# Final norm moved into the last four expert steps, expert loop in groups of step pairs: a 1-core encoder step

## The chip, the cores and the metric

One core of a Trainium2 chip runs the whole program. The metric is device time in microseconds (us). The kernel before took 2573.78 us (median of 3 runs, 2573.71 to 2576.18).

## What is computed

One layer for a prompt (2048 tokens) and a batch of samples (8 x 16 tokens), width 1024, float32: token mixing, cross-attention, a mixture of 32 SwiGLU experts, and a final RMSNorm. The part around the change, cut from the reference:

```
def rms_norm(x, g):
    y = x * lax.rsqrt(jnp.mean(x * x, axis=-1, keepdims=True) + EPS)
    return y * g

# top-1 of 4 groups, then top-2 of the 8 experts of that group
expert = g_idx * EXPERTS_PER_GROUP + top_i            # (n, 2)
y = routed_experts(t, expert, w_eg, w_eu, w_ed)       # silu(x @ w_eg[e]) * (x @ w_eu[e]) @ w_ed[e]
x = x + einsum('nk,nkd->nd', gate, y)
...
y_prompt = rms_norm(xp, g_final)
y_sample = rms_norm(xs, g_final)
```

Both experts of a token are in one group of eight.

## The kernel before

The 2176 tokens are 17 tiles of 128 rows (tile 0 in the order of work is the sample tile, then the 16 prompt tiles). The program is a row of stages; each ends with a barrier of all engines and a clearing of its semaphores (`one_stage`, L108 to L117). The last two concern us.

The router and expert stage (L1257 on). For each tile it makes x2 (input plus attention) and the normed h3, stores both to DRAM (`x2_d`, `h3_d`), routes the tokens, and writes for each of a token's two experts one row [token, gate] into `table_d` at a place that depends on expert and rank (`place`, `scatter_slots`). Then it runs the expert steps. A step has two lanes of 64 rows: the upper half of the array's columns works for an expert of 0 to 15, the lower half for one of 16 to 31 (`both`, L1992). Weights lie in three slots of 6 MB; lane 0 alternates between two, lane 1 has one, so that its next expert is loaded part by part (gate, up, down; 2 MB each, `load_part`, L1245) as the step that used it last frees each part. The loads are in the order of need on SP's queue.

In a step (`work` of each engine), TensorE multiplies gate and up, turns the next step's input (`turn_x`) and its own hidden rows (`turn_h`), and multiplies down. ScalarE does silu, half of each eviction and half of the output (`y_evac`, L1646); VectorE does the other halves. GpSimd gathers the input rows two steps ahead (`gather`, L1505), reads the pairs [token, gate] three steps ahead (`fetch`) and once more for the output (`fetch_again`), and adds the 128 output rows onto `x2_d` with an indirect accumulating DMA (`scatter`, L1515), each after the one before has landed (semaphores `y_out`).

How many steps are needed (`ns`) is known only on the device, between 34 and 84. `expert_steps` (L1370) runs steps 1 to 3 and then a loop of 40 pairs with an `If(t.v < ns)` around each step: L91 is the loop, L1378 the two conditions. In this run `ns` is 42 (steps 0 to 41): 19 pairs of the loop work and 21 are passed over.

The final norm (L2146 on) is a stage of its own: SP loads the 17 tiles of x2 (L2165), ScalarE squares and sums them (L2192), GpSimd makes rstd in two instructions (L2177, L2179), VectorE scales (L2204), SP and ScalarE store (L2169, L2187).

## Time and profile before

| | |
|---|---|
| median of 3 runs | 2573.78 us |
| the profiled execution | 2574.19 us |
| its span, first to last instruction | 2572.3 us |
| TensorE matmul busy | 2441.5 us, 95% of the span |
| VectorE, ScalarE, GpSimd busy | 859.4, 467.1, 510.7 us |
| DMA moved | 391.12 MB, mean 152 GB/s |
| expert steps | 1 to 41 from about 1573 to 2501 us, 22.62 us each |
| final stage, with what leads to it | 2501 to 2572 us |

The page divides the span into 40 slices of 64 us. TensorE stands at nine tenths or more in nearly all of them and at 8 and 0 in the last two, where DMA is at 4 and 7. So there is one stretch where the engine that bounds the program has nothing to do, and it is the end. The table says nothing of waits: those are read in the timeline.

### The profile page before, as it was taken

How to read it: one execution, taken by the hardware profiler on the slowest of the kernel's cores; microseconds unless marked ns; L12 is line 12 of the kernel's file. 1: busy time of each engine (PE TensorE's matmuls, PEld its weight loads, DVE VectorE, ACT ScalarE, POOL GpSimd, SP SyncE). 2: the span in 40 equal slices, each digit the busy share in tenths (PEclk: the TensorE clock that was granted, in tenths of full speed). 3: DMA queues.
4: the chain of work that ended last, by engine and by line, in shares of the span. 5: the costliest groups of instructions: out<-in, count | busy, mean ns of one | idle time of the engine just before them, and what ended most of it. 6: DMA issues, size and time to landing. Idle time of an engine off the chain costs nothing. (4 is left out here: it accounts for less than half of the span.)

```text
span 2572.3 us, 30380 instructions
## 1 busy us (share of the span) xinstructions
PE 2441.5 (95%) x9511; PEld 1120.5 (44%) x9512; DVE 859.4 (33%) x2312; ACT 467.1 (18%) x945; POOL 510.7 (20%) x623
## 2 busy tenths in 40 slices
PE   8999999999999988999999999999999999999980
PEld 4444444444444664555555543333333333333330
DVE  1586747566584212233333332111111111110113
ACT  2222222222121122222222211001010101010103
POOL 1122222322222000011111112211222221222214
PEclk9999999999999999999999999999999999999995
DMA  6211011110243325311111147945987297988947
GB/s 222 103 45 52 33 62 37 62 37 33 87 156 123 119 108 211 133 65 65 66 66 66 58 156 238 331 128 169 296 291 245 49 326 245 304 283 267 311 145 288
DMA packets 154278, 391.12 MB, mean 152 GB/s; under 512 B 20738, under 2 KB 21274, under 8 KB 154186
## 3 DMA queue, kind: packets, MB, share of 16 engines
q1 hardware_dynamic: 133666, 339.57, 37.1%
q0 software_dynamic: 19040, 45.23, 7.3%
q10 hardware_dynamic: 1488, 5.26, 0.5%
q8 instruction: 46, 0.75, 0.1%
q14 instruction: 38, 0.31, 0.0%
HBM read 323.53 MB, written 66.71 MB: 152 GB/s over the span
## 5 line engine op out<-in xcount | busy, mean ns | idle before, releaser
L1994 PE MATMUL r_pss<-W,r_h2T 128*64 x1312 | 571.2, 593 | 1.0 <-issue 1.0
L1995 PE MATMUL r_pss<-W,r_h2T 128*64 128x512 f32 x1312 | 571.2, 593 | 0.0
L748 PE MATMUL a_psz<-W 128*128 128x512 f32 x1088 | 481.1, 595 | 1.3 <-ACT W L506 1.3
L601 DVE SCALAR_TENSOR_TENSOR yacc<-aext,pcol,yacc 128x256 f32<-128x256 f32 x928 | 370.8, 476 | 0.3 <-issue 0.3
L1994 PEld LDWEIGHTS r_pss<-W,r_h2T 128*64 128x64 f32 x1312 | 180.0, 137 | 370.0 <-issue 370.0
L748 PEld LDWEIGHTS a_psz<-W 128*128 128x128 f32 x1088 | 203.6, 191 | 237.4 <-issue 237.4
L1994 PE MATMUL r_psx<-W,r_x1r 128*64 x656 | 290.1, 595 | 3.6
L1995 PE MATMUL r_psx<-W,r_x1r 128*64 128x512 f32 x656 | 290.3, 595 | 0.0
L1958 PE MATMUL r_psx<-W 128*128 128x512 f32 x544 | 237.6, 595 | 0.0
L1931 PE MATMUL r_pss<-W,r_h2T 128*128 128x512 f32 x512 | 226.9, 596 | 3.1 <-POOL r_tokens L1449 3.1
L1805 DVE TENSOR_TENSOR r_x1r<-r_pss,r_x1r 128x256 f32<-128x256 f32 x84 | 31.7, 419 | 530.4 <-PE r_pss L1995 504.5
L1515 POOL DMA_INDIRECT x_scratch<-r_x,e_stoken x42 | 69.4, 1653 | 643.2 <-DVE r_x L1817 319.2
L1995 PEld LDWEIGHTS r_pss<-W,r_h2T 128*64 128x64 f32 x1312 | 180.2, 137 | 0.0
L471 POOL TENSOR_TENSOR W<-W 128x512 f32<-128x512 f32 x34 | 115.3, 3397 | 268.1 <-ACT W L578 268.1
L1994 PEld LDWEIGHTS r_psx<-W,r_x1r 128*64 128x64 f32 x656 | 86.5, 137 | 174.1 <-issue 174.1
L1958 PEld LDWEIGHTS r_psx<-W 128*128 128x128 f32 x544 | 102.6, 191 | 122.6 <-issue 122.6
L1931 PEld LDWEIGHTS r_pss<-W,r_h2T 128*128 128x128 f32 x512 | 95.4, 191 | 111.5 <-issue 111.5
L916 PE MATMUL a_psz<-W,a_maT 128*128 128x512 f32 x272 | 122.3, 592 | 0.0
L916 PE MATMUL a_psz<-W 128*128 128x512 f32 x272 | 122.3, 592 | 0.0
L1817 DVE TENSOR_SCALAR r_x<-r_psx,e_spair 128x512 f32<-128x512 f32 x42 | 31.5, 750 | 260.5 <-PE r_psx L1995 258.3
L1995 PEld LDWEIGHTS r_psx<-W,r_x1r 128*64 128x64 f32 x656 | 86.5, 137 | 0.0
L1630 ACT ACTIVATE r_x1r<-r_pss 128x512 f32<-128x512 f32 x42 | 25.1, 597 | 322.8 <-PE r_pss L1995 322.7
(337 smaller groups left out, 2246.6 us busy)
## 6 DMA issues: line engine op xcount, KB each, us to landing
W<-in_w_expert_gate SPq DMA_DIRECT2D x32, 2048.0 KB, 10.8
W<-in_w_expert_up SPq DMA_DIRECT2D x32, 2048.0 KB, 9.6
W<-in_w_expert_down SPq DMA_DIRECT2D x32, 2048.0 KB, 10.6
W<-in_x_prompt SPq DMA_DIRECT2D x32, 512.0 KB, 4.2
x_scratch<-W SPq DMA_DIRECT2D x18, 512.0 KB, 3.0
r_x1r<-x_scratch SPq DMA_DIRECT2D x17, 512.0 KB, 4.3
x_scratch<-r_x SPq DMA_DIRECT2D x17, 512.0 KB, 2.9
h_scratch<-r_h SPq DMA_DIRECT2D x17, 512.0 KB, 2.9
```

Of the source, the lines that this page charges most:

```text
L471: pool.tensor_tensor(x, mixed[:, 512 * n:512 * n + 512], x, ALU.add).then_inc(S["x1_half"], 1)
L601: ins = dve.scalar_tensor_tensor(out=out, in0=src, scalar=w, in1=yacc[:, i, :], op0=ALU.mult, op1=ALU.add)
L748: last = pe.matmul(psz[bank][:], hT[t.par][:, k, :], w_in[bank][:, k, :], start=(k == 0), stop=(k == KD - 1))
L916: last = pe.matmul(psz[n][:], (maT[:, k, :] if k < CG else mbl[t.par][:, k - CG, :]), w_out[:, k, 512 * n:512 * n + 512], start=(k == 0), ...
L1515: pool.indirect_dma_start(out=x2_d.rearrange("t p d -> (t p) d"), out_offset=bass.IndirectOffsetOnAxis(ap=stoken[t.par][:], axis=0), in_=y ...
L1630: act.activation(sg[:], psg[:], ACT.Silu).then_inc(T["silu_done"], 1)
L1805: dve.tensor_tensor(hb[:, c], psu[:, c], sg[:, c], ALU.mult).then_inc(T["h_done"], 1)
L1817: dve.tensor_scalar(yb[t.par][:, 512:1024], psx[:, 512:1024], spair[t.par][:, 1:2], None, ALU.mult).then_inc(T["y_done"], 1)
L1931: last = pe.matmul(pss[:, 2 * n:2 * n + 2, :].rearrange("p h n -> p (h n)"), h2T[i % 2][:, k, :], A[:, k, 512 * n:512 * n + 512], start=(k ...
L1958: last = pe.matmul(psx[:, 512 * n:512 * n + 512], (pT if i else qT)[:, c, :], (B if i else w_xo)[:, c, 512 * n:512 * n + 512], start=(c == ...
L1994: pe.matmul(out[0:HALF, :], xt[:, 0:HALF], W[:, bass.ds(base + at, 512)], start=start, stop=stop)
L1995: return pe.matmul(out[HALF:P, :], xt[:, HALF:P], W[:, at:at + 512], start=start, stop=stop)
```

## The change

- Each row of `table_d` gets a third number: the row of the prompt output, or with 65536 added (out of range) if the token's other expert has a higher number. Of a token's two rows, only that of the later expert has a valid output row.
- Steps 1 to 3 as before. Then an outer loop over groups of 6 pairs, with a condition around the group, an inner loop over its pairs, and one condition around each pair. Then always four last steps, written out (j = 0 to 3). The device computes the number of pairs as (steps - 3) >> 1.
- In last step j ScalarE loads four tiles of x2 (behind its eviction of the next input, once all scatters of the steps before have landed), squares them in halves of 512 columns behind its half of the output eviction, and stores the normed tiles of round j-1 behind silu. VectorE adds the halves and eps and scales, in place. GpSimd makes rstd with one instruction. GpSimd's scatter of step j waits until the four loads of round j have landed.
- Tokens that one of the last four steps still changes are normed wrongly or too early in this. After the last scatter, GpSimd gathers the 4 x 128 rows of these steps again from `x2_d`, they are squared and scaled, and are written with an indirect DMA to the output rows of the third column, where out-of-range rows are dropped. The sample tile is loaded after the last scatter and normed whole.
- The final stage is gone; `g_final` is loaded by SP behind the third set of expert weights.

The core of the diff:

```
+LAST = 4
+ROUND = 4
+GROUP = 6
...
-        table_d = nc.dram_tensor("table_scratch", [NE * REG, 2], F32, kind="Internal").ap()
+        table_d = nc.dram_tensor("table_scratch", [NE * REG, 3], F32, kind="Internal").ap()
...
+            def count_pairs(eng):
                 eng.wait_ge(T["count_known"], 1)
-                return eng.value_load(count[0:1, 0:1], min_val=STEPS_MIN, max_val=STEPS_MAX)
-            def expert_steps(eng, ns, work):
-                def step(t):
-                    if isinstance(t.v, int) and t.v == 0:
-                        return
-                    if isinstance(t.v, int) and t.v < STEPS_MIN:
-                        work(t)
-                        return
-                    with eng.If(t.v < ns):
-                        work(t)
-                steps(eng, step, 4, (STEPS_MAX - 4) // 2, STEPS_MAX)
+                return eng.value_load(count[0:1, 0:1], min_val=(STEPS_MIN + 1 - LAST) // 2, max_val=(STEPS_MAX + 1 - LAST) // 2)
...
+            def expert_steps(eng, pairs, work):
+                for t in range(1, 4):
+                    work(fixed(t))
+                with eng.Fori(2, (STEPS_MAX + 1 - LAST) // 2, GROUP) as first:
+                    with eng.If(first < pairs):
+                        with eng.Fori(first, first + GROUP) as g:
+                            with eng.If(g < pairs):
+                                for u in range(2):
+                                    work(Tile(2 * g + u, g, u))
+                for j in range(LAST):
+                    work(Tile(2 * pairs + j, pairs + j // 2, j % 2), j)
...
+                    sp.wait_ge(S["h3_done"], NT)
+                    sp.dma_start(gl[:], I["g_final"].rearrange("(a d) -> a d", a=1).partition_broadcast(P).rearrange("p a d -> p (a d)")).then_inc(F["gl_here"], 16)
...
+                    pairs = count_pairs(sp)
+                    for i in range(2):
+                        sp.wait_ge(y_out[i], 16 * (pairs + LAST // 2))
+                        settle(sp)
+                    sp.wait_ge(T["h_turned"], 4 * (pairs + LAST // 2))
+                    settle(sp)
+                    sp.dma_start(sample[:], x2_d[1, :, :]).then_inc(F["sample_here"], 16)
+                    sp.wait_ge(F["out_done"], NT)
+                    sp.dma_start(O["y_s"].rearrange("b t d -> (b t) d"), sample[:]).then_inc(F["sample_out"], 16)
+                    sp.wait_ge(F["sample_out"], 16)
+                    for i in range(ROUND):
+                        sp.wait_ge(acc_out[i], 16 * LAST)
...
+                    pool.memset(place_f[:, 0, :], NOWHERE).then_inc(S["iotas"], 1)
+                    pool.iota(place_f[:, 1:NT, :], [[P, PT], [0, 2]], base=0, channel_multiplier=1, allow_small_or_imprecise_dtypes=True).then_inc(S["iotas"], 1)
...
                         need(pool, T["token_done"], t.v - 1)
+                        settle(pool)
                         fetch_pairs(t, pair[t.par], pair_here[t.par])
...
+                    pairs = count_pairs(pool)
+                    def final_rstd(n):
+                        pool.wait_ge(F["summed"], n + 1)
+                        pool.tensor_tensor(frs[:, n:n + 1], fsum[:, n:n + 1], mhalf[:], ALU.pow).then_inc(F["rstd"], 1)
+                    def work(t, j=-LAST):
+                        if j < LAST - 2:
+                            gather(t.at(2))
+                        if j < LAST - 3:
+                            fetch(t.at(3))
                         fetch_again(t)
+                        if j >= 0:
+                            pool.wait_ge(F["redo_known"], 2 * j + 2)
+                            for i in range(ROUND):
+                                pool.wait_ge(acc_here[i], 16 * (j + 1))
                         scatter(t)
-                    expert_steps(pool, ns, work)
+                        if j >= 0:
+                            for i in range(ROUND):
+                                final_rstd(ROUND * j + i)
+                    expert_steps(pool, pairs, work)
+                    final_rstd(PT)
                     for i in range(2):
-                        pool.wait_ge(y_out[i], 16 * ((ns + (1 - i)) // 2))
-                        pool.wait_ge(x_here[i], 16 * ((ns + (3 - i)) // 2))
-                        pool.wait_ge(pair_here[i], 32 * ((ns + (4 - i)) // 2))
+                        pool.wait_ge(x_here[i], 16 * (pairs + LAST // 2))
+                        settle(pool)
+                        pool.wait_ge(pair_here[i], 32 * (pairs + LAST // 2))
+                        settle(pool)
+                        pool.wait_ge(y_out[i], 16 * (pairs + LAST // 2))
+                        settle(pool)
+                    pool.wait_ge(T["x_turned"], 4 * (pairs + LAST // 2))
+                    settle(pool)
+                    pool.wait_ge(T["up_done"], 2 * (pairs + LAST // 2) + 1)
+                    settle(pool)
+                    for j in range(LAST):
+                        pool.indirect_dma_start(out=redo[j], out_offset=None, in_=x2_d.rearrange("t p d -> (t p) d"),
+                                                in_offset=bass.IndirectOffsetOnAxis(ap=redo_in[j][:], axis=0)).then_inc(redo_here[j], 16)
+                    for i in range(ROUND):
+                        pool.wait_ge(acc_out[i], 16 * LAST)
+                    final_rstd(NT)
+                    for j in range(LAST):
+                        if j + 1 < LAST:
+                            final_rstd(NT + j + 1)
+                        pool.wait_ge(F["out_done"], NT + j + 1)
+                        pool.indirect_dma_start(out=O["y_p"].rearrange("b t d -> (b t) d"),
+                                                out_offset=bass.IndirectOffsetOnAxis(ap=redo_out[j][:], axis=0),
+                                                in_=redo[j], in_offset=None, bounds_check=PT * P - 1, oob_is_err=False).then_inc(F["redone"], 16)
+                    pool.wait_ge(F["redone"], 16 * LAST)
...
+                    def final_load(j):
+                        for i in range(2):
+                            act.wait_ge(y_out[i], 16 * (pairs + (j + 1 - i) // 2))
+                            settle(act)
+                        if j == 0:
+                            act.wait_ge(S["h3T_done"], NT)
...
+                        for i in range(ROUND):
+                            need(act, acc_out[i], 16 * j)
+                            act.dma_start(acc[i], x2_d[2 + ROUND * j + i, :, :]).then_inc(acc_here[i], 16)
+                    def final_store(j):
+                        for i in range(ROUND):
+                            act.wait_ge(F["out_done"], ROUND * j + i + 1)
+                            act.dma_start(y_p[ROUND * j + i, :, :], acc[i]).then_inc(acc_out[i], 16)
+                    def square_f(n, src):
+                        for m in range(2):
+                            need(act, F["squares"], 2 * n + m)
+                            act.activation(junk_f, src[:, 512 * m:512 * m + 512], ACT.Square, scale=1 / 32,
+                                           accum_out=fss[:, n, m:m + 1]).then_inc(F["squares"], 1)
+                    def square_whole(n, src):
+                        need(act, F["squares"], PT + n)
+                        act.activation(pst[:].rearrange("p k n -> p (k n)"), src, ACT.Square, scale=1 / 32, accum_out=fss[:, n, 0:1]).then_inc(F["squares"], 1)
+                    def final_squares(j):
+                        for i in range(ROUND):
+                            act.wait_ge(acc_here[i], 16 * (j + 1))
+                            square_f(ROUND * j + i, acc[i])
+                    def work(t, j=-LAST):
                         silu(t)
+                        if j >= 1:
+                            final_store(j - 1)
                         hT_out(t)
-                        xT_out(t.at(1))
+                        if j < LAST - 1:
+                            xT_out(t.at(1))
+                        if j >= 0:
+                            final_load(j)
                         y_evac(t)
-                    expert_steps(act, ns, work)
+                        if j >= 0:
+                            final_squares(j)
+                    expert_steps(act, pairs, work)
+                    final_store(LAST - 1)
+                    act.wait_ge(F["sample_here"], 16)
+                    square_whole(PT, sample[:])
+                    for j in range(LAST):
+                        act.wait_ge(redo_here[j], 16)
+                        square_whole(NT + j, redo[j])
...
+                        for k in range(2):
+                            put(dve.tensor_tensor(sooner_f[par][:, k:k + 1], ef[par][:, k:k + 1], ef[par][:, 1 - k:2 - k], ALU.is_lt), "sooner")
+                        dve.wait_ge(S["sooner"], 2 * n)
+                        put(dve.scalar_tensor_tensor(out=val[par][:, :, 2], in0=sooner_f[par][:], scalar=NOWHERE, in1=place_f[:, i, :], op0=ALU.mult, op1=ALU.add), "rank2")
                         dve.wait_ge(S["slotf"], n)
-                        dve.wait_ge(S["rank2"], 2 * n)
+                        dve.wait_ge(S["rank2"], 3 * n)
                         put(dve.tensor_copy(slot_i[par][:], slotf[:]), "slot")
...
+                        if j >= 0:
+                            dve.tensor_copy(redo_in[j][:], spair[t.par][:, 0:1]).then_inc(F["redo_known"], 1)
+                            dve.tensor_copy(redo_out[j][:], spair[t.par][:, 2:3]).then_inc(F["redo_known"], 1)
...
+                    then(dve.tensor_tensor(most[:], end[0:1, EPL - 1:EPL], end[0:1, NE - 1:NE], ALU.max))
+                    then(dve.tensor_scalar(most_i[:], most[:], float(1 - LAST), None, ALU.add))
+                    dve.tensor_scalar(count[:], most_i[:], 1, None, ALU.arith_shift_right).then_inc(T["count_known"], 1)
...
+                    def final_sum(n):
+                        if n < PT:
+                            dve.wait_ge(F["squares"], 2 * n + 2)
+                            dve.tensor_scalar(fsum[:, n:n + 1], fss[:, n, 0:1], fss[:, n, 1:2], EPS, ALU.add, ALU.add).then_inc(F["summed"], 1)
+                        else:
+                            dve.wait_ge(F["squares"], PT + n + 1)
+                            dve.tensor_scalar(fsum[:, n:n + 1], fss[:, n, 0:1], EPS, None, ALU.add).then_inc(F["summed"], 1)
+                    def final_scale(n, tile):
+                        dve.wait_ge(F["rstd"], n + 1)
+                        if n == 0:
+                            dve.wait_ge(F["gl_here"], 16)
+                        dve.scalar_tensor_tensor(out=tile, in0=tile, scalar=frs[:, n:n + 1], in1=gl[:],
+                                                 op0=ALU.mult, op1=ALU.mult).then_inc(F["out_done"], 1)
+                    def work(t, j=-LAST):
+                        if j < LAST - 2:
+                            tokens(t.at(2))
                         hidden(t)
                         hT_out(t)
-                        xT_out(t.at(1))
-                        y_evac(t)
-                    expert_steps(dve, ns, work)
+                        if j < LAST - 1:
+                            xT_out(t.at(1))
+                        y_evac(t, j)
+                        if j >= 0:
+                            final_sum(ROUND * j)
+                            for i in range(ROUND):
+                                if i + 1 < ROUND:
+                                    final_sum(ROUND * j + i + 1)
+                                final_scale(ROUND * j + i, acc[i])
+                    expert_steps(dve, pairs, work)
+                    final_sum(PT)
+                    final_scale(PT, sample[:])
+                    final_sum(NT)
+                    for j in range(LAST):
+                        if j + 1 < LAST:
+                            final_sum(NT + j + 1)
+                        final_scale(NT + j, redo[j])
...
+                    def work(t, j=-LAST):
...
+                        more = j < LAST - 1
+                        if more:
+                            turn_x(t.at(1), (0, 1, 2, 3))
                         turn_h(t, 0)
-                        turn_x(t.at(1), (4, 5))
+                        if more:
+                            turn_x(t.at(1), (4, 5))
                         turn_h(t, 1)
-                        turn_x(t.at(1), (6, 7))
+                        if more:
+                            turn_x(t.at(1), (6, 7))
...
-        with one_stage() as st:
...
```

## Rows read from the trace of the kernel before

**Rows 1.** Windows; columns: stretch, its length, busy of each engine, PEclk, DMA share, GB/s.

```profile
2500.00:2524.00 24.00, 1.61 (x8) 0.30 (x4) 0.75 (x1) 0.69 (x1) 1.65 (x1) 0.58 0.15 22
2524.00:2572.00 48.00, 0.00 (x0) 0.00 (x0) 21.83 (x17) 19.54 (x34) 30.56 (x34) 0.50 0.96 383
```

**Rows 2.** Timeline, 2501 to 2567 us: start, length, engine, line, idle before in brackets.

```profile
2501.01 0.59 PE L1995 MATMUL r_psx<-W,r_x1r 128*64 128x512 f32 x1
...
2501.65 0.75 DVE L1817 TENSOR_SCALAR r_x<-r_psx,e_spair 128x512 f32<-128x512 f32 x1 [6.32 <-PE r_psx L1995]
...
2503.31 1.65 POOL L1515 DMA_INDIRECT x_scratch<-r_x,e_stoken  x1 [15.58 <-DVE r_x L1817]
...
2531.17 1.06 ACT L2192 ACTIVATE f_junk<-W 128x1024 f32<-128x1024 f32 x1 [0.30 <-DMA W<-x_scratch]
...
2564.30 0.57 POOL L2179 TENSOR_TENSOR f_rs<-f_rs,mhalf 128x1 f32<-128x1 f32 x1
...
2564.90 1.28 DVE L2204 SCALAR_TENSOR_TENSOR W<-W,f_rs,f_gfinal 128x1024 f32<-128x1024 f32 x1 [0.77 <-POOL f_rs L2179]
...
2566.21 0.34 SPq L2169 DMA_DIRECT2D out_y_s<-W  x1
```

**Rows 3.** Lines L1378 and L1382 after 2499.6 us: count, ns min/median/max, first and last start.

```profile
L1378 PEldq COMPARE_BRANCH  x38: 208/208/208, 2499.9 to 2520.4; - x38
...
L1378 POOLq COMPARE_BRANCH  x42: 45/45/50, 2503.5 to 2520.4; - x42
...
L1382 POOLq DRAIN  x1: 1621/1621/1621, 2521.6 to 2521.6; - x1
...
L1382 SPq EVENT_SEMAPHORE  x1: 17/17/17, 2523.4 to 2523.4; - x1
```

**Rows 4.** TensorE's queue at a pair boundary: start of a step's first issue and matmul.

```profile
L1994 PEldq FUSED_REGOPS  x6: 37/46/51, 2455.0 to 2456.2; - x6
...
L1994 PE MATMUL r_pss<-W,r_h2T x1: 592/592/592, 2456.2 to 2456.2; 128*64 x1
```

**Rows 5.** Windows of two clock drops, and of step 39; columns as in rows 1.

```profile
1514.20:1521.00 6.80, 4.99 (x15) 3.71 (x16) 3.47 (x16) 2.23 (x3) 1.85 (x2) 0.50 0.48 129
1558.50:1561.90 3.40, 3.40 (x10) 0.98 (x8) 0.90 (x4) 0.00 (x0) 1.13 (x2) 0.51 0.76 291
2433.57:2456.19 22.62, 22.49 (x111) 8.31 (x109) 2.65 (x7) 2.16 (x4) 4.86 (x6) 1.00 0.96 323
```

**Rows 6.** Timeline: TensorE's gap before 1515 us, and SP's last gate load.

```profile
1515.32 0.64 PE L1976 MATMUL r_psk<-r_picked,r_lower 128*128 128x32 f32 x2 [2.63 <-DVE r_picked L1749]
...
2441.01 0.39 SPq L1254 DMA_DIRECT2D W<-in_w_expert_gate  x1
```

**Rows 7.** DMA, 2441 to 2457 us: KB each, us from issue to landing.

```profile
W<-in_w_expert_gate SPq DMA_DIRECT2D x1, 2048.0 KB, 10.8
```

**Rows 8.** DMA by queue: packets, MB, share of 16 engines; 2539 to 2541 us.

```profile
q1 hardware_dynamic: 123, 0.44, 54.7%
q10 hardware_dynamic: 89, 0.36, 44.2%
```

**Rows 9.** DMA to landing: alone, last scatter (2503), last gather (2482), sample store (2566).

```profile
x_scratch<-r_x,e_stoken POOLq DMA_INDIRECT x1, 6.4
...
r_x1n<-h_scratch,e_token POOLq DMA_INDIRECT x1, 6.2
...
out_y_s<-W SPq DMA_DIRECT2D x1, 512.0 KB, 5.3
```

**Rows 10.** Router tail, timeline: the last slots, and TensorE's wait for step 1's input.

```profile
1550.51 0.17 DVE L1777 CAST r_slot<-r_slotf 128x2 int32<-128x2 f32 x1
...
1569.80 1.97 PE L1983 MATMUL r_pst<-ident,r_x1n 128*128 128x128 f32 x8 [2.93 <-DMA r_x1n<-h_scratch,e_token]
```

**Rows 11.** Instruction fetches, TensorE's queue (q8): 1573 to 1700, then 1575 to 2500 us.

```profile
q8 instruction: 5, 0.08, 0.3%
...
q8 instruction: 5, 0.08, 0.0%
```

122 lines of the change are left out of this document (44 added, 78 removed).

## The prediction

> **What bounds the kernel now.** I read the windows first, then the timeline of the end, then the sequencers. Until 2500 us TensorE is busy almost without a break. Behind it, 24 us hold next to no work of any kind and 48 us hold the final stage with DMA at 0.96 of its time [rows 1]. The timeline says what these 72 us are [rows 2]: the last matmul ends at 2501.6, VectorE's half of the output at 2502.4, the last scatter starts at 2503.3, and it lands 6.4 us later [rows 9], at 2509.7. The stage still ends only at 2523.4. What fills the time is the loop over pairs that are not wanted: TensorE passes 38 conditions from 2499.9 to 2520.4, 37 intervals of 0.554 us, so 1.11 us for a pair of them, and GpSimd's 42 last until 2520.4 too; then come GpSimd's drain of 1.62 us and the barrier [rows 3]. From last matmul to the end of the span (2572.3) it is 70.7 us. This is what the change can win. The other question is what it puts in front of the last matmul, for there every microsecond of TensorE's idleness is one of the kernel's: step 39 takes 22.62 us, of which TensorE is busy 22.49, and DMA is already at 0.96 and 323 GB/s in it [rows 5].
>
> **The tail after the change.** I lay it out on the clock of before, from the same last matmul. The last scatter lands at 2509.7, as above. SP then loads the sample tile, 512 KB; the same size stored alone takes 5.3 [rows 9]: 2515.0. A square of 1024 columns is 1.06 [rows 2], 1.3 with its sum's read-out and handover; VectorE's small sum and GpSimd's power, 0.57 [rows 2], with their handovers 1.1: 2517.4. This stands in front of the gathers on GpSimd's queue, and so do eight waits with an increment each; I estimate 1.7 us: 2519.1. The first gather lands after 6.2 [rows 9]: 2525.3. The scale of tile 0 stands behind the sum of tile 1, so two squares (2.6) and the small steps (0.6) come first: 2528.5. Scale 1.28, then 0.9 from VectorE's end to the indirect DMA's start, as between 2502.4 and 2503.3 [rows 2]: 2530.7. GpSimd does for each further tile a power (0.57) and an issue of between 1.0 and 1.65 (the scatter's row) with gaps, about 2.3: the fourth starts at 2537.6. It lands after between 5.3 (plain) and 6.4 (accumulating) [rows 9]; it is plain, so 5.3: 2542.9. Drain and both barriers: 1.8 us from the drain's start to SP's release [rows 3] and about 1 for the second: 2545.7. Against 2572.3 the tail wins 26.6 us. The fourth round's four stores run beside the scatter's landing and cost nothing; without that cover they would be some 5 us. VectorE's scales, 17 x 1.28 of before, and the squares of rounds 0 to 2 lie behind the output evictions, where both engines wait for TensorE for most of a step (VectorE is busy 2.65 and ScalarE 2.16 of 22.62 us [rows 5]); a round adds 8 half squares, about 7 us, and four scales, about 6. That is covered as long as the tiles are there in time.
>
> **What stands in front of the last matmul.**
> 1. Router tail. In `place` three more instructions stand before the cast of the slots (at 1550.51), some 0.4 us by their neighbours' pitch. The slots' scatter, the pairs' fetch and the gather hang on it, and TensorE waits 2.93 us for that gather [rows 10]: the 0.4 is exposed. The 512 KB of `g_final` behind the third weights may hold small packets up by a little more: 0.7 together, bounds 0.2 and 2. The longer plan (two more dependent instructions before `begin`) ends before VectorE needs the turned table; free. The other `place` calls, the table's larger fill at the start and the two settings for the third column lie beside a busy TensorE or in waits: 0, at most 0.5.
> 2. Group boundaries. TensorE's queue issues a step's first product at 2455.0 and the product starts at 2456.2 [rows 4]: a lead of 1.15 us, of which I take 0.45 as the way from issue to start, so 0.7 to spare. A group boundary (two of them) adds three register and branch steps, 0.85: 0.15 idle each, 0.3 in all. One condition for a pair instead of two gives nothing, as it was covered.
> 3. Entry into the last four steps. Five passed blocks remain (one pair, four groups), and they now stand between steps 37 and 38. A block has two taken branches instead of three, so 1.11 x 2/3 = 0.74 and 3.7 for five, 3.5 more than a usual boundary: 2.8 us idle after the 0.7. A gap of 2.63 us [rows 6] was followed by 6.8 us at half the clock, 1.2 GHz, and another stretch of 3.4 us at half also followed a wait [rows 5]. In such a stretch half the time is lost: 1.7 to 3.4. I take 1.7, bounds 0 and 3.4. Together 4.5.
> 4. DMA in steps 38 to 40. Round 0's loads (2.1 MB) go out near 2427, its stores near 2442 to 2447, round 1's loads near 2450. Lane 1 changes its expert before step 40: the gate part is issued at 2441.0 and lands 10.8 us later [rows 6, 7], at 2451.8, 4.4 us before the product that needs it [rows 4]. In that window DMA is full; 4.2 MB more at the 400 GB/s that two queues reach together (0.80 MB in 2 us [rows 8]) are 10.5 us. If everything is delayed alike, TensorE idles 10.5 - 4.4 = 6.1 us. But the queues take turns by packets: 123 to 89 packets of like size [rows 8]. The gate's rows are 2 KB and those of x2 are 4 KB, so beside them the gate gets a third of the bytes and lands behind nearly all of both: 8.5 by my count. I take 7, bounds 0 and 11, and 2.5 for the clock behind such a gap. Queued behind on ScalarE is silu of step 40, and on GpSimd the scatter of step 39; both have over 4 us before TensorE needs them.
>
> The Trainium skill, DMA: Bandwidth & Descriptors, Queues, rings and completion order, says that each DMA engine goes round the queues that have work and takes a whole packet from one before it switches. By that rule the third holds and item 4 is 8.5 rather than 6.1, the sum 2563.7 rather than 2561.3; rows 8 agree for packets of one size, and no row shows two sizes side by side on these two queues.
>
> **Sum.** 26.6 - 0.7 - 0.3 - 4.5 - 9.5 = 11.6 us won. The span would be 2560.7; with the 1.9 us that lie around it in the profiled execution (2574.19), 2562.6. That execution was 0.4 above the median of 2573.78, so for the median 2562.2.
>
> **Rivals.**
> - The transfers are hidden (chance 15%). For: the weights are the older requests, steps 38 and 40 have room, and later stores would slip past the critical load. Against: rows 5, DMA at 0.96. Items 4 and the clock's part go: 2562.2 - 9.5 = 2552.7.
> - The corrected rows cost more (12%). Here every indirect DMA takes what it takes in the loop beside other traffic, and four at once hold one another up: 3.2 more for the last scatter, 2.7 for the gathers, 4 for the writes, 9.9 in all: 2572. For: the gathers and writes are four of 512 KB each. Against: nothing else is in flight there.
> - Slower: TensorE fetches its instructions anew at each jump back (8%). The four steps written out lengthen the code behind the loop by twice the body. TensorE's fetches were five of 16 KB each, all before 1700, and none from there to 2500 [rows 11]: 17 more passes went without. If the longer code pushes the body out, each of the 17 pairs waits for a fetch; at 1.7 us beyond the 0.7 of lead this is 29 us, and the time 2591. It decides from 1.0 us a pair (11.6 + 5.1, over 17). Against: the first pass through the code needed fetches and the later ones none, and the program before wrote out three steps ahead of its loop without harm.
> - It doesn't do what it says (in the forecast's spread). Loads of round j wait for scatter j-1, scatter j waits for loads j: two latencies of 8 to 10 us in 22.6. Were they longer, ScalarE would stand at the loads and hold its half of the output: some us in step 39 or 40 alone.
>
> The Trainium skill, Runtime: NRT & Kernel Launch, Instruction fetch mechanics, says that a taken branch to a block outside the window stops the engine for a fetch, and that TensorE's memory is 128 KiB. By that rule a body of two steps stays inside and the rival costs nothing.
>
> **How the numbers follow.** The forecast's own case (62%) spans 2556 to 2570 by the bounds of items 3 and 4. A rest of 3% is slower for reasons not listed. The range of 2549 to 2577 takes in the hidden transfers with the clock's part gone too, and the longer corrected rows. A difference of under 0.2% (5.1 us) is what a measurement of this kernel can hardly tell from none. Faster by more (below 2568.6): 57 + 15 + 5 = 77%. Within: 5 + 7 + 1 = 13%. Slower: 10%.
>
> **What would show it.** Tail: last matmul to the end of the span 44 us instead of 70.7, with a string of four indirect writes 2.3 us apart. Entry: TensorE idle near 3 us between steps 37 and 38, then half clock. Item 4: a gap at the gate product of step 40, released by a DMA, and none at 41. Fetch: the step's 22.6 us longer, and fetches up to 2400. Wrong would be a gap at step 39 or 40 released by ScalarE, or landings of the indirect DMAs near 10 us in the tail.

## The result and the profile after

The changed kernel takes 2556.44 us (median of 4 runs, 2556.15 to 2560.85), beside 2574.16 for the kernel before on the same chip: a ratio of 0.9935, 95% interval 0.9922 to 0.9948. The forecast was 2562.2 with a range of 2549 to 2577. The profiled execution has a span of 2554.6 us, 17.7 less than before.

To set the two spans side by side I took the start of each expert step (its first gate product) from both traces:

| event, us | before | after | later by |
|---|---|---|---|
| step 1 | 1572.75 | 1574.58 | +1.8 |
| step 4 | 1641.71 | 1643.79 | +2.1 |
| step 37, the last in the loop | 2388.31 | 2387.65 | -0.7 |
| step 38, first of the last four | 2410.93 | 2412.59 | +1.7 |
| step 39 | 2433.56 | 2435.26 | +1.7 |
| step 40 | 2456.19 | 2463.59 | +7.4 |
| step 41 | 2478.81 | 2489.67 | +10.9 |
| last matmul ends | 2501.61 | 2512.19 | +10.6 |
| end of the span | 2572.3 | 2554.6 | -17.7 |

So the last matmul comes 10.6 us later, and what stands behind it takes 42.4 us instead of 70.7, which wins 28.3. This is the shape that was forecast (15.0 later, 26.6 won). The windows answer rows 1 and 5: stretch, length, busy of TensorE, its weight loads, VectorE, ScalarE and GpSimd, then clock, DMA share and GB/s, for step 39, step 40, step 41 and the tail.

```profile
2435.26:2463.59 28.33, 25.14 (x110) 9.38 (x108) 8.50 (x17) 7.13 (x19) 6.98 (x8) 0.88 1.02 369
2463.59:2489.67 26.08, 22.71 (x110) 8.08 (x108) 8.35 (x16) 9.15 (x24) 5.95 (x7) 1.00 1.00 346
2489.67:2512.20 22.53, 21.76 (x102) 7.30 (x98) 7.75 (x15) 7.67 (x20) 5.93 (x7) 1.00 0.74 243
2512.20:2554.60 42.40, 0.00 (x0) 0.00 (x0) 13.30 (x19) 10.44 (x24) 19.38 (x18) 0.55 0.53 172
```

Step 39 is 5.7 us longer than in rows 5 and runs at a mean clock of 0.88; step 40 is 3.5 longer at full clock; DMA is full in both. Step 41, where DMA has room, costs nothing. TensorE's timeline has these gaps in the last four steps; the bracket is the idle time before the matmul and what ended it.

```profile
2412.59 0.64 PE L2161 MATMUL r_pss<-W,r_h2T 128*64 x1 [2.31 <-issue]
2452.94 0.69 PE L2172 MATMUL r_psr<-ident,r_x1r 128*128 128x128 f32 x2 [3.19 <-DVE r_x1r L1937]
2472.94 0.64 PE L2161 MATMUL r_pss<-W,r_h2T 128*64 x1 [2.32 <-DMA W<-in_w_expert_up]
2481.65 0.44 PE L2172 MATMUL r_psr<-ident,r_x1r 128*128 128x128 f32 x2 [1.04 <-DVE r_x1r L1937]
2504.10 0.44 PE L2172 MATMUL r_psr<-ident,r_x1r 128*128 128x128 f32 x2 [0.52 <-DVE r_x1r L1937]
```

The first is the entry and the third a transfer, the up part of step 40. The second is no transfer, although one was forecast next: in step 39 TensorE waits for its own hidden rows. VectorE's side of it (timeline; ScalarE's last square, GpSimd's scatter and rstd, VectorE's first and last scale, the hidden rows):

```profile
2444.37 0.63 ACT L1765 ACTIVATE r_x1r<-f_acc 128x512 f32<-128x512 f32 x1
2444.68 1.64 POOL L1561 DMA_INDIRECT x_scratch<-r_x,e_stoken  x1 [22.87 <-issue]
2445.78 1.68 POOL L1602 TENSOR_TENSOR router_w<-router_w,mhalf 128x1 f32<-128x1 f32 x2
2446.97 1.28 DVE L2055 SCALAR_TENSOR_TENSOR r_h<-r_h,router_w,r_gffn 128x1024 f32<-128x1024 f32 x1 [6.38 <-POOL router_w L1602]
2451.21 1.28 DVE L2055 SCALAR_TENSOR_TENSOR f_acc<-f_acc,router_w,r_gffn 128x1024 f32<-128x1024 f32 x1
2452.47 0.74 DVE L1937 TENSOR_TENSOR r_x1r<-r_pss,r_x1r 128x256 f32<-128x256 f32 x2
```

GpSimd's scatter of step 38 waits for the four loads of round 0. Its row names no releaser, but without the rounds (`e3_no_rounds`, below) the same scatter starts at 2437.6 instead of 2444.7. The rstd of all four tiles stand behind that scatter, the four scales behind the rstd, and the hidden rows of step 39 behind the scales. The loads land late, since they go beside the weights; of round 0's fourth load and of the gate and up parts of step 40 (KB, us from issue to landing; before, a gate part took 10.8 [rows 7]), and the first stores of round 0, which go out behind the scales:

```profile
f_acc<-x_scratch ACTq DMA_DIRECT2D x1, 512.0 KB, 13.8
...
W<-in_w_expert_gate SPq DMA_DIRECT2D x1, 2048.0 KB, 15.7
...
W<-in_w_expert_up SPq DMA_DIRECT2D x1, 2048.0 KB, 23.3
...
2448.28 1.67 ACTq L1760 DMA_DIRECT2D out_y_p<-r_h  x2
```

The tail, in order: last scatter, sample load, first gather, first and last indirect write.

```profile
2513.90 1.65 POOL L1561 DMA_INDIRECT x_scratch<-r_x,e_stoken  x1 [8.36 <-DVE r_x L1952]
...
2520.34 0.35 SPq L1476 DMA_DIRECT2D r_x1r<-x_scratch  x1
...
2529.35 1.18 POOL L1632 DMA_INDIRECT r_x1n<-x_scratch,f_redo_in  x1 [1.08 <-issue]
...
2539.80 1.75 POOL L1641 DMA_INDIRECT out_y_p<-r_x1n,f_redo_out  x1 [0.47 <-issue]
...
2547.50 0.97 POOL L1641 DMA_INDIRECT out_y_p<-r_h2T,f_redo_out  x1 [0.30 <-issue]
```

### The profile page after: what moved, and what is told of

Read it like the earlier page. It is cut to its first block, busy times and chain, and to the rows that moved or that the text cites. A ratio compares the mean times of both kernels' runs of the same rounds, so it can differ in the third digit from the quotient of the medians.

```text
span 2554.6 us, 29787 instructions
## 1 busy us (share of the span) xinstructions
PE 2443.8 (96%) x9503; PEld 1122.2 (44%) x9504; DVE 872.8 (34%) x2395; ACT 476.0 (19%) x984; POOL 503.9 (20%) x613
## 4 chain that ended last, share of the span: by engine, by line
PE 56%; DMA 2%; issue 1%; POOL 1%; DVE 1%; POOLq 0%; ACT 0%; ACTq 0%; DVEq 0%
PE r_pss L2161 20%; PE r_psx L2161 11%; PE r_psx L2125 9%; PE r_pss L2098 9%; PE r_pst L2150 2%; PE r_psr L2134 1%; DMA f_acc<-x_scratch 1%; PE r_pst L2117 1%; PE r_psr L2172 1%; PE r_pss L2162 1%; PE r_pst L2090 1%; PE r_pst L2107 1%; DMA out_y_p<-f_acc 0%; POOL router_w L1602 0%; PE r_psk L2172 0%
## 6 DMA issues: line engine op xcount, KB each, us to landing
W<-in_w_expert_gate SPq DMA_DIRECT2D x32, 2048.0 KB, 10.9
```

## Experiments

Executions of one kernel mostly lie within 5 us of each other (once, seven of the kernel before, within 8: 2568.19 to 2576.20), so differences under that are read from the steps of the profiled executions and not from the medians. The profiled executions differ in what they lose ahead of step 1 and in half clock; that this is what spreads the others was not shown. In all tables, "steps 39 + 40" is the time from the start of step 39 to that of step 41 (54.4 us in the changed kernel), and "tail" is from the end of the last matmul to the end of the span (42.4).

### Which part of the change brings the gain

`e1_loop_only`, on the kernel before:

```
...
-                steps(eng, step, 4, (STEPS_MAX - 4) // 2, STEPS_MAX)
+                with eng.Fori(2, (STEPS_MAX + 1 - LAST) // 2, GROUP) as first:
+                    with eng.If(first < pairs):
+                        with eng.Fori(first, first + GROUP) as g:
+                            with eng.If(g < pairs):
+                                for u in range(2):
+                                    work(Tile(2 * g + u, g, u))
+                for j in range(LAST):
+                    work(Tile(2 * pairs + j, pairs + j // 2, j % 2))
```

> The kernel before with one part of the change alone: the loop in groups of 6 pairs with one condition for a pair, the last four steps written out, the count as pairs. Everything else, the final stage too, is as before. From the two traces: the loop is 2.7 us shorter (22.54 instead of 22.62 us a step), the five passed blocks ahead of step 38 cost 2.3, so the last matmul ends near 2501. But nothing is passed over behind it any more: the last scatter lands near 2509.3 and the final stage starts 3.7 us later, 11.4 us sooner than before. If that is all, the time is 2562.5 and two thirds of what the change gained are the loop's and not the final norm's. Rival (the final norm inside the steps brings the gain): within 3 us of the kernel before.

Measured: 2563.43 us, ratio 0.9957 (0.9940 to 0.9974). The windows behind the last matmul (columns as above):

```profile
2503.23:2515.00 11.77, 0.00 (x0) 0.00 (x0) 0.75 (x1) 0.00 (x0) 1.65 (x1) 0.65 0.30 45
2515.00:2562.70 47.70, 0.00 (x0) 0.00 (x0) 21.84 (x17) 19.54 (x34) 30.70 (x34) 0.50 0.97 385
```

The final stage is as long as in rows 1, and the stretch between it and the last matmul is 11.8 us instead of 22.4: the passed pairs of rows 3 are gone from behind the last matmul. Over half of the gain comes from the loop: 0.0043 of 0.0065 by the ratios (two thirds, with wide intervals), 9.6 of 17.7 us by the spans of the profiled executions. The tail is 59.5, so that 11.2 of the 28.3 us that the tail became shorter are the loop's, and 17.1 are the final norm's, of which steps 39 and 40 take more than half back.

`e2_one_condition`, on the kernel before:

```
-                    with eng.If(t.v < ns):
-                        work(t)
...
+                with eng.Fori(2, STEPS_MAX // 2) as g:
+                    with eng.If(2 * g < ns):
+                        for u in range(2):
+                            work(Tile(2 * g + u, g, u))
```

> The kernel before with one edit: one condition around the two steps of a pair instead of one around each (right for the even number of steps of this input), no groups, nothing written out but steps 1 to 3. Theory: the 0.08 us a step that the changed loop is shorter comes from this alone, so the steps take 22.54 us instead of 22.62 and the last matmul ends 3.1 us sooner; each of the 21 passed pairs costs TensorE 0.73 us instead of 1.11, so the final stage starts 8.6 us sooner than before: 2565.2. Rival (the shorter steps come with the grouped loop, the condition only shortens the passed pairs): steps of 22.62, the stage 5.5 to 8 us sooner, 2566 to 2568.5.

Measured: 2567.09 us, ratio 0.9972 (0.9961 to 0.9984). The time lies in the rival's range, but the steps are the theory's. Steps 4 to 37 take 22.542 us each on average, as in the changed kernel (22.541), against 22.624 before: every second step is 22.45 instead of 22.62. So the shorter steps come from the single condition; groups and written-out steps have no part in them. Where no condition at all stands between two steps (39 and 40 of `e1_loop_only`), both take 22.45. In the changed kernel the 0.17 us of a short step appear near the turned hidden rows and not at its start. Why is not settled. The end was over-estimated: the tail is 65.9, 4.8 shorter, where I had expected 5.5.

`e8_group12`, on the changed kernel:

```
-GROUP = 6
+GROUP = 12
```

> The changed kernel with groups of 12 pairs instead of 6: 3 blocks are passed over ahead of step 38 (one pair, two groups) instead of 5, and there is one group boundary instead of two. Theory (a passed block is 0.73 us and stands in front of TensorE): the gap at the start of step 38 is 0.85 us instead of 2.31, the time 1.5 less, 2555. Rival (the gap is the way into the written-out steps, whatever is passed): the gap stays at 2.3 and the time at 2556.4.

Measured: 2561.6 us, ratio 0.9948 (0.9931 to 0.9966), 5 us slower than the changed kernel. The count in the expectation is wrong. The inner loop runs over a whole group, so that with 19 pairs the second group (14 to 25) passes seven pairs; with the two groups behind it 9 blocks are passed and not 3. TensorE's conditions of passed pairs and groups, and the start of step 38 (count, ns, first and last start; then the timeline):

```profile
L1403 PEldq COMPARE_BRANCH  x7: 208/208/208, 2404.1 to 2408.4; - x7
...
L1401 PEldq COMPARE_BRANCH  x2: 208/208/208, 2409.4 to 2410.1; - x2
...
2414.05 1.11 PE L2161 MATMUL r_pss<-W,r_h2T 128*64 x1 [5.98 <-issue]
```

In the changed kernel the same rows are one pair and four groups:

```profile
L1403 PEldq COMPARE_BRANCH  x1: 208/208/208, 2406.3 to 2406.3; - x1
...
L1401 PEldq COMPARE_BRANCH  x4: 208/208/208, 2407.2 to 2409.5; - x4
```

A passed block is (2408.4 - 2404.1) / 6 = 0.72 us and stands in front of TensorE: four more of them are 2.9 of the 3.7 us by which the gap grew. Behind the gap of 5.98 the clock fell to 1.2 GHz (the matmul takes 1.11 us instead of 0.64; the mean granted clock of the next 5.95 us is 0.61), and step 38 took 24.98 instead of 22.67. The theory holds, with its sign turned by my count. The other 0.8 us stand behind the last passed condition: from its start to the matmul it is 3.95 us (2410.1 to 2414.05) instead of 3.1; why is open.

### What holds TensorE in steps 39 and 40

`e3_no_rounds` leaves the work of the rounds out:

```
-                            for i in range(ROUND):
-                                pool.wait_ge(acc_here[i], 16 * (j + 1))
...
-                            final_load(j)
...
-                            final_squares(j)
```

> The changed kernel without its four rounds over the 16 prompt tiles: no loads, squares, sums, rstd, scales and stores in the last four steps, and no wait of the scatter for the loads. The prompt output is left unwritten but for the corrected rows; the sample tile and the corrected rows are normed as before. Theory 1 (read from the trace of after: step 39 waits 3.2 us for VectorE, which is behind the scales of round 0, and loses some 2.5 us to half clock; step 40 waits 2.3 us for its up weights and 1.0 for VectorE): steps 39 to 41 are 22.6, 22.6 and 22.5 us, the last matmul 9.2 us earlier, the time 2547.2. Rival (the written-out steps or the passed blocks ahead of them cost it, not the rounds): 2554 or more. The tail from the last matmul on stays near 42.4 in both.

Measured: 2544.24 us. Steps 39 and 40:

```profile
2435.78:2458.23 22.45, 22.43 (x110) 8.32 (x108) 2.77 (x9) 2.16 (x4) 3.80 (x4) 1.00 0.95 324
2458.23:2480.68 22.45, 22.44 (x110) 8.32 (x108) 2.71 (x8) 2.16 (x4) 2.76 (x3) 1.00 0.43 123
```

Without the rounds both steps are free of gaps; 54.4 - 44.9 = 9.5 us are the rounds' price there. The gap of 2.3 ahead of step 38 stays. Step 39 has DMA at 0.95 of its own, and step 40 at 0.43. The tail is 40.1, 2.3 shorter than expected: the last scatter takes 6.2 us as in the changed kernel, but the sample tile comes 3.6 us after its load instead of 6.0, with the stores of the fourth round gone from beside it.

Two readings of the 9.5 us were then open. By Q, VectorE's queue is the cost. By D, the bytes are, and the wait for VectorE only hides a later one. `e4_transfers_only` keeps the bytes and leaves the arithmetic out:

```
-                            act.wait_ge(F["out_done"], ROUND * j + i + 1)
+                            act.wait_ge(acc_here[i], 16 * (j + 1))
...
-                            final_squares(j)
...
-                                final_scale(ROUND * j + i, acc[i])
```

> The rounds keep their loads and stores, and the scatter its wait for the loads, but the squares, sums, rstd and scales of the 16 prompt tiles are left out: the tiles are stored as loaded. Theory Q (VectorE's queue is the cost, 3.2 + 2.5 + 1.0 us): the gaps at the turned hidden rows are gone, the 2.3 at the up part stay, 2549.7. Theory D (DMA supply is the cost, and the stall in step 39 only gave it time): the up part of step 40 lands near 2472 as before while TensorE wants it from 2464.7, so that the gap there grows to 6 to 8 us, and the time is 2554 to 2556.

`e5_rstd_first` keeps all the work and frees VectorE in time:

```
+                            for i in range(ROUND - 1):
+                                final_rstd(ROUND * j + i)
                             for i in range(ROUND):
                                 pool.wait_ge(acc_here[i], 16 * (j + 1))
                         scatter(t)
                         if j >= 0:
-                            for i in range(ROUND):
-                                final_rstd(ROUND * j + i)
+                            final_rstd(ROUND * j + ROUND - 1)
```

> The changed kernel with one order changed: GpSimd makes rstd of the first three tiles of a round before it waits for the four loads and starts the scatter; the fourth follows the scatter. VectorE is then done with three scales by the time it now begins, and takes the hidden rows of step 39 at their usual time. Theory Q: no gap of 3.2 us in step 39 and none of 1.0 in step 40, no half clock, 2.3 at the up part stay: 2549.7. Theory D: the up part lands near 2472 all the same and TensorE waits there 6 to 8 us instead of 2.3: 2554 to 2556.

Measured: 2552.63 us for e4 and 2557.06 for e5. Steps 39 + 40 are 53.5 and 53.8 us, where Q wanted 47.7 and the changed kernel has 54.4. The gaps at the hidden rows are gone in both, and in both one gap stands in their place, at the gate part of step 40. Of e5, TensorE's timeline, the transfer of that gate part (then the same of e3), and, of the window from there on, the clock (columns: stretch, length, TensorE busy, clock, DMA share, GB/s):

```profile
2463.68 1.11 PE L2162 MATMUL r_pss<-W,r_h2T 128*64 x1 [5.90 <-DMA W<-in_w_expert_gate]
...
W<-in_w_expert_gate SPq DMA_DIRECT2D x1, 2048.0 KB, 20.8
...
W<-in_w_expert_gate SPq DMA_DIRECT2D x1, 2048.0 KB, 11.8
...
2463.68:2470.00 6.32, 6.32 (x18) 0.55 1.04 398
```

D holds by the steps (by the times alone it would not be settled: its range was 2554 to 2556, and e4 lies 1.4 us under and e5 1.1 over it), and this is item 4 of the forecast as it was written: the gate part lands 20.8 us after its issue, 11.8 in e3, TensorE waits 5.9 us for it, and half clock follows. Not foreseen by D either was the place: I had expected it at the up part. In the changed kernel the wait for VectorE does two things. It stands ahead of the gate part and gives it time, and it holds the stores of round 0 back, which go out from 2448.3 instead of 2443.0 in e5. So the gate part, issued within 0.1 us of the same time in both, lands 15.7 us after its issue, at 2458.4, and not at 2463.4, and it is the up part that TensorE waits for (2.3 us). Taken away, the wait comes back as one for DMA: the same bytes stand in front of another part. What separates e4 from e5 lies outside these steps: e5's tail is 45.4 us, 4.3 longer than e4's and 3.0 longer than that of the changed kernel, since three rstd now stand in front of its last scatter.

Rows of e5 also show that the entry can cost more than in the profiled execution of the changed kernel: after the same gap of 2.31 us, step 38 took 24.37 us with a clock of 0.64 at its start.

### Taking the cost away

`e7_both_orders` adds to e5, on GpSimd:

```
                     expert_steps(pool, pairs, work)
-                    final_rstd(PT)
...
                     for i in range(ROUND):
                         pool.wait_ge(acc_out[i], 16 * LAST)
+                    final_rstd(PT)
                     final_rstd(NT)
```

> As the run before, and GpSimd issues the four gathers of the corrected rows before the rstd of the sample tile, which now stands in front of them (first gather 2529.4, while the last scatter has landed by 2520.3). Both theories: the first gather starts near 2521, its rows land near 2527, the sample's rstd is not later; the first indirect write starts near 2532 instead of 2539.8. So 7 to 8 us less than the run before, 2542 by theory Q and 2547 to 2549 by theory D. Rival: the gathers collide with the sample's load and the stores of the fourth round, and 3 us or less are won.

Measured: 2552.78 us. The tail is 40.4 instead of e5's 45.4: 5.0 us won, short of the 7 to 8. The gathers wait for the last scatter, which starts 5.0 us behind the last matmul instead of 1.7 and lands 8.6 us later instead of 6.2; the next run moves it.

`e9_last_scatter_first`:

```
-                            for i in range(ROUND - 1):
+                            for i in range(ROUND - 1 if j < LAST - 1 else 0):
                                 final_rstd(ROUND * j + i)
...
-                            final_rstd(ROUND * j + ROUND - 1)
+                            for i in range(ROUND - 1 if j < LAST - 1 else 0, ROUND):
+                                final_rstd(ROUND * j + i)
```

> As e7_both_orders, but in the last of the four steps GpSimd starts the scatter first and makes all four rstd behind it, as the changed kernel does. In e7 three rstd stood in front of that scatter (2515.24, 5.0 us behind the last matmul, instead of 1.7), and it landed after 8.6 instead of 6.2 us beside the stores of the fourth round. Expected: scatter 1.7 behind the last matmul, 3.3 us won, and 2 more if it lands alone: tail 35 to 37 instead of 40.4, time 2547.5 to 2549.5. Rival (what stands behind the scatter is bound by the four rstd and stores): the tail stays at 40.

Measured: 2551.7 us (2548.24 to 2552.72), ratio 0.9915 (0.9899 to 0.9932). The profiled execution, the fastest of the four, has a tail of 36.7 us, as expected; the median gained only 1 us on e7 and doesn't settle it.

`e10_early_load`, on ScalarE:

```
                     def work(t, j=-LAST):
+                        if j == 0:
+                            final_load(0)
                         silu(t)
```

> As e9, and ScalarE issues the four loads of round 0 ahead of silu of step 38 instead of behind the eviction of its next input: near 2421 instead of 2428 us, where DMA stands nearly idle for 3 us. Theory D (bytes ahead of the gate part of step 40 hold it up): some 1.3 to 1.6 MB of the 2.1 go into the idle stretch, so the gate lands some 3.5 us sooner, the gap of 5.6 us at it falls to about 2 and its half clock goes, 4 to 6 us won: 2542 to 2544. Part comes back if the loads of round 1 then meet the up part. Rival (only the loads of round 1 and the stores of round 0 count, which are not moved): the gap stays at 5.6.

Measured: 2550.72 us (2548.85 to 2553.3), ratio 0.9912 (0.9894 to 0.9930). Steps 39 + 40 are 54.1 us, no less than in e9 (53.7), and the gap at the gate part is 7.1 us:

```profile
2463.38 1.11 PE L2165 MATMUL r_pss<-W,r_h2T 128*64 x1 [7.07 <-DMA W<-in_w_expert_gate]
```

A miss. What had been held up by the loads (scatter, stores, and so the next loads) moved ahead together with them: round 1's loads went out at 2449.0 instead of 2454.9 in e9, straight into the gate part's way. The rival's half was right, that it is those bytes that count.

`e11_after_up` keeps them out of the way, and `e12_after_gate` half as long (`gate_here` in place of `up_here`):

```
...
+                        if 1 <= j < LAST - 1:
+                            wanted = act.value_load(steps_row[0:1, 3, bass.ds(t.at(1).v, 1)], min_val=16, max_val=16 * NE)
+                            act.wait_ge(up_here, wanted)
+                            settle(act)
                         if j >= 1:
                             final_load(j)
```

> As e10, and ScalarE issues the loads of rounds 1 and 2 only when the up part of the next step has landed (a wait on the weights' own semaphore ahead of them). Theory D: gate and up of step 40 then share DMA with the stores of round 0 alone, the gaps at both are under 1 us, steps 39 to 41 are near 22.5 each as in the kernel without rounds, the last matmul ends near 2503.5 and the time is 2541. Rival (the later loads come to stand in front of silu or the scatter): a gap of 2 us or more at the turned hidden rows of step 40 or 41, released by ScalarE or VectorE, and 2544 or more.

> As e11, but the loads of rounds 1 and 2 wait for the gate part of the next step instead of its up part. In e11 the loads of round 1 began at 2465.5, and silu of step 40, behind their squares on ScalarE, came at 2477.6, which held TensorE for 7.1 us; its gate gap, though, was 2.3 us without half clock instead of 7.1 with it. Theory: gate near 2460 again, loads from 2460, silu of step 40 near 2471, before hidden rows are wanted near 2473; the up part shares DMA with them and costs 0 to 3. Steps 39 and 40 together 48.5 to 50.5 us instead of 54.1, time 2545 to 2547. Rival (what is taken off the gate is paid at up or at silu in full): 53 or more for the two, 2549 or more.

Measured: 2553.57 and 2553.34 us. The gap at the gate part of step 40 falls to 2.3 and 2.4 us, at full clock; the one at the up part is gone. But steps 39 + 40 are 56.5 and 56.2 us. Both rivals came true, and the row that shows it is ScalarE's silu of step 40 in e12, behind eight halves of squares that wait for their tiles, and the matmul that waited:

```profile
2467.77 0.63 ACT L1768 ACTIVATE r_x1r<-r_h 128x512 f32<-128x512 f32 x1 [4.97 <-DMA r_h<-x_scratch]
...
2477.09 0.58 ACT L1713 ACTIVATE r_x1r<-r_pss 128x512 f32<-128x512 f32 x1
...
2480.83 0.69 PE L2181 MATMUL r_psr<-ident,r_x1r 128*128 128x128 f32 x2 [6.10 <-DVE r_x1r L1946]
```

`e13_gate_group12` is e12 with GROUP = 12.

> As e12_after_gate, with groups of 12 pairs. Theory: both act apart from each other, 1.5 less than e12. Rival (what the entry gives back, the gate of step 40 takes, since it lands when DMA lets it): the gap there grows by the same 1.5 and the time is that of e12.

Measured: 2558.76 us, 5.4 more than e12, from the same wrong count as e8. The question it was for is answered with the other sign: the gap ahead of step 38 grew by 3.6 us and its clock fell, and the gap at the gate part did not shrink (2.63 against 2.39). What the entry costs is not given back later.

The best version run is e10 (0.9912) with e9 (0.9915) beside it; the changed kernel has 0.9935. The intervals overlap, so that they are faster than it by 5 us is likely and not certain.

## Why the forecast was near

The terms of the sum, as forecast and as the two traces have them (us won, losses with a minus; the measured ones add up to 17.7 before rounding):

| term | forecast | measured |
|---|---|---|
| tail behind the last matmul | 26.6 | 28.3 |
| item 1, router tail | -0.7 | -0.1 |
| one condition for a pair | 0 | 2.7 |
| item 2, group boundaries | -0.3 | in the 2.7 |
| item 3, entry | -4.5 | -2.3 |
| item 4, steps 38 to 40 | -9.5 | -9.2 |
| step 41 | 0 | 0.3 |
| what stands ahead of 1015 us | 0 | -1.9 |
| sum | 11.6 | 17.7 |

**Tail.** The string of steps came as laid out. From the end of the last matmul: first gather at 17.2 us (forecast 17.5), first indirect write at 27.6 (29.1), the fourth at 35.3 (36.0), end at 42.4 (44.1). The last term was too large because the indirect writes land 3.4 to 4.4 us after issue, not 5.3. That the corrected rows cost 9.9 more is refuted: the last scatter lands after 6.2 us, the gathers after 5.5 to 5.9. One assumption of this term was wrong without being seen in its sum: the stores of the fourth round were to cost nothing, but they run beside the sample's load, which takes 6.0 us with them and 3.6 without (e3).

**The term that was missing.** I put the single condition at nothing, "as it was covered" by the lead of TensorE's queue in rows 4. e2 shows it to be worth 0.08 us a step, 2.8 over 34 steps. The step that failed is the conclusion from a covered queue at the step's start to the whole step: 22.62 in rows 5 was never explained down to TensorE's busy 22.49, and that was the sign.

**Entry.** Idle 2.31 us where 2.8 was forecast, by blocks of 0.72 instead of 0.74 and a longer lead; e8 confirms that blocks are what is paid, and no instruction fetch of TensorE falls between 2385 and 2430. The 1.7 for half clock did not come in the profiled execution and did in e5's (24.37 against 22.67). It is a term that some executions have, so that it was lost or saved by luck. Its basis was also read too long: of the 6.8 us at half clock in rows 5, 1.1 lie in the gap itself.

**Steps 38 to 40.** The size was right (9.2 against 9.5), the place was not. "A gap at the gate product of step 40, released by a DMA" is what e4, e5, e7, e9 and e10 show, with 5.4 to 7.1 us and half clock behind it; the changed kernel itself shows 3.2 us at the hidden rows of step 39, then half clock, 2.3 at the up part of step 40 and 1.0 at its hidden rows. What I had named as wrong if seen, a gap in step 39 or 40 released by ScalarE, is there with VectorE in its place. The step that failed is the sentence that the scales are "covered as long as the tiles are there in time": I had costed the loads at DMA's full rate, and did not follow a late load through scatter, rstd and scales to the hidden rows, each of them first in some engine's queue. That it cost the forecast nothing was luck: I had not seen that both waits stand in line for the same late bytes. The sum says so: with VectorE's wait, 54.4 us; without it, 53.8.

**Router tail.** The three instructions did delay the cast of the slots, by 0.3 us (0.74 us behind the start of the instruction before them instead of 0.41). How much of it TensorE sees doesn't show: its gap for the gather is 3.07 us, 2.93 before, but 2.48 in e5 with the same code. And the gap ahead of the last tiles' ranks, which I had taken as covered, is 2.99 instead of 2.63 [rows 6]; less half clock afterwards returned it. By step 4 the sum is 0.1.

**Instruction fetches.** The slower rival needed fetches up to 2400. TensorE's fetch queue between 1575 and 2500 us, and between 2385 and 2513:

```profile
q8 instruction: 8, 0.13, 0.1%
...
q8 instruction: 4, 0.07, 0.2%
```

There is none between 1710 and 2380, and the last four steps fetch their own code without a gap that TensorE shows. The rule of the Trainium skill (Runtime: NRT & Kernel Launch, Instruction fetch mechanics), by which a body of this size stays inside, agrees with that.

**Turns of whole packets.** In item 4 this rule of the Trainium skill (DMA: Bandwidth & Descriptors, Queues, rings and completion order) stood for 8.5 us of idle time at the gate product, and an even delay for 6.1. The idle time there is 5.4 to 7.1 us (5.9 in e5), nearer to the even delay, but stores and loads went out at other times than laid out, so the runs decide neither. The 8.5 does not come out of the item's own numbers either: it means a landing 8.5 + 4.4 = 12.9 us late, and the 4.2 MB take 10.5. Measured, e5's gate part takes 9.0 us more than e3's.

The total is 6.1 us better than forecast by the condition (2.7), the entry (2.2), the tail (1.7), items 1, 2 and 4 (1.2) and step 41 (0.3), less the 1.9 ahead of 1015 us (rounded terms). The first 1.1 of these stand ahead of 1000 us, where the change touches only the fill of the table, the rest at the start of the router stage, where GpSimd makes two more constants. Among the later runs that have the same code there, step 1 starts anywhere from 1572.5 (e8) to 1575.0 (e3), so I take the 1.9 as a difference between executions; that it is one is not shown. All large errors but this one ran the same way, and the measured median stands at the lower edge of the forecast's own case (2556 to 2570).

## What to carry to other kernels

Before a large part is moved into a loop that one engine bounds, see what the empty passes of that loop cost behind the last step: here a change of the loop alone gave over half of the gain. Where DMA was full in a step, bytes put into it were paid there in every order tried (steps 39 + 40: 53.4 to 56.5 us, against 44.9 without them), and moving the wait from one engine to another showed only who waits; the time came from the tail, where nothing else ran. A wait that is taken away should be replaced in thought by the next one in line (e5), and a transfer that is held back by whoever stands behind it in the issuing engine's queue (e11, e12).

## What the runs showed of the hardware

- Whether half clock follows a short gap is not fixed. Of the gaps of 2.30 to 2.39 us in the last steps, twelve were followed by full clock (1.00) and one by half (2.31 in e5, mean 0.64 in the 4.7 us behind it). Gaps of 2.63 us were followed by half clock in rows 6 and by full clock in e13 (1.00 in the 5.4 us behind it). Behind all twelve gaps of 3.19 to 7.07 us in the last steps the clock fell (mean 0.50 to 0.65 in the 3 to 6 us behind them).
- An rstd on GpSimd takes 0.57 us alone and up to 1.5 while VectorE scales, and an indirect write 0.97 us alone and 2.03 then (the changed kernel's tail).
- One transfer of 2 MB took from 9.6 us (median of the up parts in the kernel before) to 23.3 (the up part of step 40 in the changed kernel) from issue to landing, by what ran beside it and was queued ahead of it.
